# Sixteen passes of two 64-row blocks become twelve passes of 32-row blocks in a mixture-of-experts stage with streamed weights

## What is computed

```python
def hier_moe(h, w_group, w_router, w_gate, w_up, w_down):
    t = h.reshape(-1, d)
    g_probs = jax.nn.softmax(t @ w_group, axis=-1)
    g_sel = jnp.argmax(g_probs, axis=-1)                       # best of 4 groups
    ...
    top_p, top_i = lax.top_k(jax.nn.softmax(e_logits, axis=-1), 2)
    weights = g_w * top_p / jnp.sum(top_p, axis=-1, keepdims=True)
    ...
    a = jnp.einsum('td,edf->tef', t, w_gate)                   # 1024 -> 256, each expert
    u = jnp.einsum('td,edf->tef', t, w_up)
    hid = jax.nn.silu(a) * u * gates[:, :, None]
    y = jnp.einsum('tef,efd->td', hid, w_down)                 # 256 -> 1024
```

## Time and profile before

| | us |
|---|---|
| median of 3 runs | 1253.07 |
| lowest and highest | 1249.19, 1253.59 |
| the profiled execution | 1254.93 |
| its span, first to last instruction | 1253.1 |

### The profile page before, as it was taken

How to read it: one execution, slowest core, us unless ns; L and a number is a source line. 1 busy time by engine, 2 the same in 40 slices (tenths; PEclk the granted TensorE clock), 3 DMA queues, 4 the chain that set the end, 5 groups by cost and what they waited for, 6 DMA issues and landing times.

```text
span 1253.1 us, 15422 instructions
## 1 busy us (share of the span) xinstructions
PE 1160.0 (93%) x5840; PEld 716.7 (57%) x5840; DVE 486.5 (39%) x869; ACT 258.5 (21%) x503; POOL 234.9 (19%) x168
## 2 busy tenths in 40 slices
PE   4999999999999999779999888989998889999993
PEld 4889889889888777533333333444444533333331
DVE  6301431431456401632321217574576352222126
ACT  4122132132133111101110012231434100111111
POOL 5332233233245330030000005500000120000004
PEclk8999999999999999889999999999999979999997
DMA  6141142141141113856999964210030575999925
GB/s 274 67 152 56 64 150 69 50 168 51 51 168 35 68 67 134 369 174 222 352 343 366 356 198 138 88 47 1 1 134 1 212 304 161 351 345 353 325 65 218
DMA packets 38354, 211.30 MB, mean 169 GB/s; under 512 B 5312, under 2 KB 5440, under 8 KB 29328
## 3 DMA queue, kind: packets, MB, share of 16 engines
q1 hardware_dynamic: 21168, 151.26, 33.4%
q10 hardware_dynamic: 12384, 42.12, 10.4%
q0 software_dynamic: 4736, 17.04, 3.7%
HBM read 307.78 MB, written 34.73 MB: 273 GB/s over the span
## 4 chain that ended last, share of the span: by engine, by line
PE 79%; DVE 12%; ACT 3%; issue 2%; DMA 2%; POOL 1%; ACTq 1%; POOLq 0%; DVEq 0%
PE ps L781 27%; PE ps L1018 17%; PE ps L1037 9%; PE ps L906 4%; PE ps L1142 3%; PE ps L1084 2%; PE ps L1006 2%; PE ps L787 2%; DVE arena L2015 2%; DVE arena L2012 2%; DMA xT<-slot_rows 2%; PE ps L995 1%; PE ps L850 1%; PE ps L956 1%; ACT arena L1447 1%
## 5 line engine op out<-in xcount | busy, mean ns | idle before, releaser
L1018 PE MATMUL ps<-ring,xT 128*64 128x512 f32 x640 | 229.1, 605 | 5.9 <-DVE xT L1487 5.9
L781 PE MATMUL ps<-x_hi,ring_r 128*128 128x264 f32 x1024 | 191.7, 287 | 2.5 <-DVE xT L1487 2.5
L2095 POOL TENSOR_TENSOR ring_r<-ring,ring_r 128x1024 fp32r<-128x1024 f32 x56 | 134.8, 2422 | 273.2 <-ACT ring_r L1234 273.2
L1018 PE MATMUL ps<-arena,xT 128*64 128x512 f32 x384 | 169.1, 593 | 0.0
L781 PEld LDWEIGHTS ps<-x_hi,ring_r 128*128 128x128 f32 x1024 | 161.0, 190 | 3.1 <-issue 2.9
L1487 DVE TENSOR_TENSOR xT<-ps,gains 128x512 f32<-128x512 f32 (+1 forms) x92 | 57.3, 665 | 252.0 <-PE ps L1006 244.0
L781 PE MATMUL ps<-xT_r,ring_r 128*128 128x264 f32 x512 | 146.5, 286 | 0.0
L1037 PE MATMUL ps<-arena 128*64 128x512 f32 x512 | 122.1, 620 | 6.4 <-ACT arena L1360 6.4
L1018 PEld LDWEIGHTS ps<-ring,xT 128*64 128x64 f32 x640 | 72.6, 139 | 94.2 <-issue 90.4
L781 PE MATMUL ps<-ring_r,x_hi 128*128 128x512 f32 x320 | 100.7, 395 | 0.0
L781 PEld LDWEIGHTS ps<-xT_r,ring_r 128*128 128x128 f32 x512 | 97.4, 190 | 0.1
(11 more groups left out here) (258 smaller groups left out, 1560.8 us busy)
## 6 DMA issues: line engine op xcount, KB each, us to landing
ring<-in_w_gu SPq DMA_DIRECT2D x46, 2048.0 KB
arena<-in_w_down SPq DMA_DIRECT2D x74, 1024.0 KB
arena<-in_w_gu SPq DMA_DIRECT2D x28, 2048.0 KB
ring<-in_w_ret SPq DMA_DIRECT2D x48, 512.0 KB, 3.6
xT<-slot_rows ACTq DMA_DIRECT2D x60, 256.0 KB, 10.2
slot_out<-arena ACTq DMA_DIRECT2D x60, 256.0 KB, 7.1
slot_rows<-arena ACTq DMA_DIRECT2D x8, 1024.0 KB, 4.2
ring<-in_w_ret_out SPq DMA_DIRECT2D x16, 512.0 KB, 4.5
```

Source lines behind the costliest of these rows:

```text
L781: last = mm(dst, a_parts[x], b_parts[y], start=(start and n == 0), stop=(stop and n == 2))
L1018: last = mm(ps[cols, b, :], xgT[:, k % 2, c, cols], by_row(gu(j))[:, c, :], start=(c == 0), stop=(c == KT - 1))
L2095: G.tensor_tensor(w_lo[slot][:, m], w_raw[slot][:, m], w_hi[to][:, m], ALU.subtract).then_inc(lo_made, 1)
```

## The change

Blocks are of BLK = 32 rows. Two of them that lie side by side are a "pair" (64 rows), and an expert with an odd number of blocks gets a "single". There are 16 pairs and 16 singles. A pass still takes 128 rows, four blocks, each in its own 32 columns of the array. `PAIRS_IN_PASS` says how many of them come in pairs; ROUNDS is 12:

- passes 0 and 1: pairs 0, 1 and pairs 2, 3
- pass 2: singles 0, 1 and pair 4; pass 3: singles 2, 3 and pair 5; pass 4: pairs 6, 7
- passes 5, 6, 7: singles 4, 5 and pair 8; singles 6, 7 and pair 9; pairs 10, 11
- passes 8, 9, 10: singles 8, 9 and pair 12; singles 10, 11 and pair 13; pairs 14, 15
- pass 11: singles 12 to 15

Weights have six buffers. Slots 0, 1, 2, 4, 5 are guessed. Slot 3 lies over `xn` (its down part in a buffer of its own, `down_rows`), and is filled by SP after the scatter and after the first rows have been read. When the singles j of a pass are done, SP loads pair j + 6 into their slot. The conditional loads for singles whose expert isn't their pair's move from SP to POOL's queue, with semaphores of their own (`gu_again`, `down_again`). The second half of `w_q` is loaded only after the last gather of layer 0, and the attention's tables in pass 11 and not in pass 8.

```diff
-BLK = 64
+BLK = 32
+PAIR = 2 * BLK
-W_SLOTS = 5
+W_SLOTS = 6
+ROWS_SLOT = 3
+GUESSED = [4, 5, 0, 1, 2]
-PASSES = [(("first", 0), ("first", 1)),
-          *((("second", k - 1), ("first", k + 1)) for k in range(1, EXPERTS - 1)),
-          (("second", EXPERTS - 2), ("second", EXPERTS - 1))]
+PAIRS_IN_PASS = (2, 2, 1, 1, 2, 1, 1, 2, 1, 1, 2, 0)
+def passes():
+    out, pairs, singles = [], 0, 0
+    for n in PAIRS_IN_PASS:
+        out.append([("single", singles + i) for i in range(4 - 2 * n)] + [("pair", pairs + i) for i in range(n)])
+        pairs, singles = pairs + n, singles + 4 - 2 * n
+    return out
...
         def gu(k):
-            s = k % W_SLOTS
-            return ring[:, (s + 1) % RING] if s < RING else gu_arena[:, s - RING]
+            return {0: ring[:, 0], 1: gu_arena[:, 0], 2: gu_arena[:, 1], 3: gu_rows, 4: ring[:, 1], 5: ring[:, 2]}[k % W_SLOTS]
...
+        def tiles_of(k):
+            at = 0
             for kind, j in PASSES[k]:
+                for _ in range(width(kind) // BLK):
+                    yield slice(at, at + BLK), j
+                    at += BLK
+        def weights_arrived(eng, pairs_in, singles_in, l, k):
+            for kind, j in PASSES[k]:
+                if kind == "pair":
+                    pair_arrived(eng, pairs_in, l, j)
+                else:
+                    singles_arrived(eng, singles_in, l, pass_of("pair", j))
...
                 sp.wait_ge(mo[l]["eb_ready"], 1)
-                for j in range(W_SLOTS):
+                for j in sorted(GUESSED):
                     guess_arrived(sp, gu_in, l, j)
                     guess_arrived(sp, down_in, l, j)
-                    e, wanted = first_of(j), first_wanted(j)
+                    e, wanted = expert_of(j)
                     gate_up_weights(l, j, e, cond=wanted)
                     down_weights(l, j, e, cond=wanted)
+                e, wanted = expert_of(ROWS_SLOT)
+                sp.wait_ge(mo[l]["scattered"], 16 * 2 * (5 - l))
+                fl.wait_full(sp, f"X0_{l}")
+                gate_up_weights(l, ROWS_SLOT, e, cond=wanted)
+                down_weights(l, ROWS_SLOT, e, cond=wanted)
+                chosen = {}
                 for k in range(ROUNDS):
+                    following = [j + W_SLOTS for kind, j in PASSES[k] if kind == "single" and j + W_SLOTS < EXPERTS]
+                    for j in following:
+                        chosen[j] = expert_of(j)
                     round_full(sp, l, gu_bank(k), k)
-                    next_weights(gate_up_weights, k)
+                    for j in following:
+                        e, wanted = chosen[j]
+                        gate_up_weights(l, j, e, cond=wanted)
                     beside(k)
                     if k:
                         round_full(sp, l, B_YB, k - 1)
-                        next_weights(down_weights, k - 1)
+                        for kind, j in PASSES[k - 1]:
+                            if kind == "single" and j + W_SLOTS < EXPERTS:
+                                e, wanted = chosen[j + W_SLOTS]
+                                down_weights(l, j + W_SLOTS, e, cond=wanted)
...
                     for c in range(KT):
-                        for cols, j in halves_of(k):
+                        for cols, j in tiles_of(k):
                             last = mm(ps[cols, b, :], xgT[:, k % 2, c, cols], by_row(gu(j))[:, c, :],
...
+                chosen = {}
+                for k in range(ROUNDS):
+                    behind, chosen = chosen, {j: single_of(j) for kind, j in PASSES[k] if kind == "pair"}
+                    if chosen:
+                        round_full(pool, l, gu_bank(k), k)
+                        singles_weights(load_gate_up, gu_again, k, chosen)
+                    if behind:
+                        round_full(pool, l, B_YB, k - 1)
+                        singles_weights(load_down, down_again, k - 1, behind)
                 pool.wait_ge(m["gather_ready"], 1)
```

More of the change, by code:

```diff
@@ L46 @@
+PASSES = passes()
 ROUNDS = len(PASSES)
-SECONDS = EXPERTS * BLK
-SLOTS = 2 * EXPERTS * BLK
-LATE = SECONDS + (EXPERTS - 2) * BLK
+SINGLES = EXPERTS * PAIR
+SLOTS = EXPERTS * (PAIR + BLK)
+LATE = SLOTS - 4 * BLK
 def pass_of(kind, j):
-    return next(p for p, halves in enumerate(PASSES) if (kind, j) in halves)
+    return next(p for p, units in enumerate(PASSES) if (kind, j) in units)
 def last_use(slot):
-    return max(pass_of("second", j) for j in range(slot, EXPERTS, W_SLOTS))
+    return max(pass_of("single", j) for j in range(slot, EXPERTS, W_SLOTS))
@@ new lines, in width, with row_groups, groups_until @@
+def width(kind):
+    return PAIR if kind == "pair" else BLK
+def row_groups(k):
+    groups, at = [], 0
+    for kind in ("single", "pair"):
+        units = [j for name, j in PASSES[k] if name == kind]
+        if units:
+            w, first = width(kind), units[0] * width(kind) + (SINGLES if kind == "single" else 0)
+            groups.append((slice(at, at + w * len(units)), slice(first, first + w * len(units))))
+            at += w * len(units)
+    return groups
+def groups_until(k, first):
+    return 16 * sum(len(row_groups(p)) for p in range(first, k + 1) if p % 2 == k % 2)
@@ L62, in most_blocks @@
 def most_blocks(tokens):
     return max((2 * tokens + (BLK - 1) * m) // BLK for m in range(2, EXPERTS + 1))
-assert most_blocks(POS) <= 2 * EXPERTS and ROUNDS % 2 == 0
-assert all(pass_of("first", j) < pass_of("second", j) for j in range(EXPERTS))
-assert all(pass_of("second", j - W_SLOTS) < pass_of("first", j) for j in range(W_SLOTS, EXPERTS))
+assert most_blocks(POS) <= 3 * EXPERTS and ROUNDS % 2 == 0
+assert PASSES[0] == [("pair", 0), ("pair", 1)] and PASSES[-1] == [("single", EXPERTS - 4 + n) for n in range(4)]
@@ L70 @@
+assert all(pass_of("pair", j) < pass_of("single", j) for j in range(EXPERTS))
+assert all(pass_of("single", j - W_SLOTS) < pass_of("pair", j) for j in range(W_SLOTS, EXPERTS))
 THRESH = (POS - 1) // BLK + 1
@@ L322, in build @@
         gu_arena = cv(2, KT * 512)
-        down = cv(W_SLOTS, 2, D)
+        down_arena = cv(5, 2, D)
         yo = cv(2, D)
@@ new lines, in first_weights @@
+            def first_weights(l, ready):
+                for j in ready:
+                    ready[j]()
+                    gate_up_weights(l, j, j)
+                rest = [j for j in (0, 1, 2, 4, 5) if j not in ready]
+                for j in rest[:2]:
+                    gate_up_weights(l, j, j)
+                for j in range(2):
+                    down_weights(l, j, j)
+                for j in rest[2:]:
+                    gate_up_weights(l, j, j)
+                for j in (2, 4, 5):
+                    down_weights(l, j, j)
```

179 lines of the change are left out of this document (85 added, 94 removed).

## The result

The changed kernel takes **1186.32 us** (median of 4 runs, 1184.5 to 1187.7), the kernel before 1252.84 beside it: ratio 0.9474, 95% interval 0.9451 to 0.9496, so 66.5 us less. Forecast were 1198 us and 55 less: the direction held, and the time lies inside the likeliest case's own range of 1182 to 1210 us. The profiled execution has a span of 1186.0 us against 1253.1, and these 67.1 us are what the profile can explain.

The account below looks back on a forecast made before the run. TensorE bounds the kernel almost end to end, with DMA nearly a limit. First layer 32.6 us less and second 22.7, weight waits, clock, slot 3 and POOL included, together 55.3: 1197.8 us; eight in ten 1158 to 1225.

Parts of the forecast that it names:

- likeliest case: Whole kernel: 1198 us, own range 1182 to 1210 us, chance 0.57.
- Passes and tiles: Expert stages: sixteen passes become twelve, four column tiles of 32 side by side, matmul factor 1.0, a pass keeps its length.
- Weights: SP's queue, full throughout, needs 104.1 us a layer; TensorE waits at gate/up 4, 7, 10 and downs 4, 7.
- 4.7 us of a pass to the rows: DMA queue in the expert stages: an expert's weights take 7.1 us, rows the rest; eight passes of rows make 37.6 us.
- Rival A: Rows move at the weights' rate, 2.4 us a pass, waits nearly vanish, TensorE limits again: 1150 to 1163 us; chance 0.10.
- weight waits, passes 4 to 10: Expert stages: pass 10 begins at 688.0 in the first layer, against about 668.5 at which TensorE would like to begin.
- slot 3: Pass 1: SP issues this load after five guesses and two more reads; wait of 0 us first layer, 3 us second.
- cold gate/ups behind waits: Gate/up after TensorE's wait before pass 10 runs partly at 1.2 GHz: 1.9 us a layer.
- POOL's skipped loads: Singles' loads, read, tested and signalled on POOL, cost 1 us a layer, 0 to 3, at the stage's end.
- pass 11's gate/up to the stage's end: Stage's end: kept as in the kernel before, 19.8 us in the first layer and 19.5 in the second.
- Clock: Waits in passes 4 and 7 pass their cold gate/up into the DMA wait behind; only pass 10's counts, 1.9 us.
- Tail: End of each expert stage: the kernel before's time carried over, 735.26 to 755.0, 19.8 us, in the first layer.

Follow-up runs that it names:

- the version one pass behind: Changed kernel with PAIRS_IN_PASS (2, 1, 2, 1, 1, 2, 1, 1, 2, 1, 2, 0), several singles one pass behind their pair, not two: 1160.88 us, ratio 0.9271.

## Why the prediction was right, and where it was off

**Passes and tiles**: right. Gate/up 6.87 us, pass 11.7 to 12.1 us, factor 1.0, shown by itself in the kernel before.

**Weights**: the mechanism was right, and three of the five places (gate/up of 7 and 10, down 4); at gate/up 4 and at down 7 there was no wait. The size was not right. The term that was mis-sized is the rows', "which leaves 4.7 us of a pass to the rows", taken for all eight passes: 37.6 us of queue, where the runs put 29.7, or 3.7 us a pass. Two faults lie in it. It took what was left over of TensorE's pace for a price of the queue, though before's pace doesn't fall when a third of the weights' bytes go. And it took every pass's rows as cut in two, where those of passes 4, 7 and 10 now go whole. By the two prices estimated above the second makes 6.3 of the 8 us and the first 1.6; no run separates them.

These 8 us came off pass 10's start. Another 3.4 came off the wait because TensorE's own way there was that much longer than forecast (1.9 for the cold gate/up of pass 7, 1.5 for the passes with a small transpose), so the waits came out as 8.0 and 8.3 us for 19.5. Rival A (2.4 us a pass) was too low by 1.3 us, a little more than the forecast was too high: in this kernel its gain doesn't come, with the rows joined (2.6 us a pass) nearly all of it does, and in the version one pass behind the queue's price is mostly covered.

**The other terms**, first and second layer, measured less forecast, from the chains above:

| term | forecast | measured | difference |
|---|---|---|---|
| weight waits, passes 4 to 10 | 19.5, 19.5 | 8.0, 8.3 | -11.5, -11.2 |
| slot 3 (wait, and a cold gate/up in the second) | 0, 3 | 2.7, 6.5 + 2.1 | +2.7, +5.6 |
| cold gate/ups behind waits | 1.9, 1.9 | 3.8, 3.8 | +1.9, +1.9 |
| POOL's skipped loads | 1, 1 | 0, 0 | -1, -1 |
| pass 11's gate/up to the stage's end | 19.8, 19.5 | 17.1, 17.0 | -2.7, -2.5 |
| sum | | | -10.6, -7.2 |

Against the stages' measured ends, counted from their first product, that leaves 0.0 and 0.3 us. It does so partly by luck: TensorE was ready for pass 1 1.6 and 1.5 us earlier than forecast, and took about 1.5 us longer from there to pass 10, waits and cold clock apart. **Slot 3**: counted from the stage's first product its load was issued 2.6 and 1.1 us later than forecast, where I had carried over SP's steps of before, and TensorE was ready for it some 1.5 us earlier. In the first layer the lateness is that of SP's first step, 5.8 us here and 2.8 in most of the profiles. **Clock**: I counted one cold gate/up a layer, that of pass 10; that of pass 7 was to vanish in the wait behind it. Both are cold, and the table counts both. Whether the 1.9 us of pass 7 were paid or only took the place of as much waiting at pass 10 isn't shown by any run. **Tail**: the last down projection of before was itself slow (5.06 and 5.37 us, 3.7 now), and the wait ahead of it was 1.3 and 0.8 us longer; I carried both over. **Outside the stages**: the forecast had nothing for the 6.3 us lost there. The errors pull both ways: of the 11.5 us between 1197.8 and 1186.3 the weight waits alone make 22.7.

## What to carry over

A DMA share of 1.0 gives no price by itself: here it stood beside 345, 368, 385 and 424 GB/s. Before pricing anything by such a stretch, ask whether the rate would fall if fewer bytes were wanted, and whether the transfers are cut there as they will be in the changed kernel; take the price from a stretch in which the engine does wait, or keep both ends in the range. Where a queue is short by a few microseconds over a stage, look for the time in which it stood idle first: here one pass of earlier release, one line in a table, brought as much as halving the loads. Transfers that share the DMA engines with others cost by how they are cut as well as by bytes: with the same bytes the time was 15.7 us longer with the row DMAs halved and 21.9 shorter with them joined. And when a wait is moved ahead on a queue, count who needs what now stands behind it.

## What I had not expected of the hardware

- Four column tiles of 32 take the slot of one full-width matmul over a whole gate/up (6.87 us with 64 records of four tiles or 32 of two), and the weight loads of 113 ns hide even where four of them are longer than the slot.
- The mixed traffic of weights and 4 KB rows goes at 368, 385 or 424 GB/s with a DMA share of 1.01 or 1.02 each time, by how the rows are cut into DMAs.
- The first of SP's table steps in the first layer's stage took 5.0 to 5.8 us in three profiled executions and 2.8 in the others, against 1.9 for the later steps; what it is wasn't found.
